# A head's sum of squares by two rounded products instead of one plain product, one slot later

## The chip, the cores and the metric

The kernel runs on one core of one Trainium2 chip. The metric is the device time of one execution in microseconds, from a few runs of the same program. Five engines work beside each other: TensorE (PE, with its weight loads as PEld), VectorE (DVE), ScalarE (ACT), GpSimd (POOL) and SyncE (SP), which issues the transfers.

## The reference

The program computes two blocks for 512 tokens of width 1024 in f32. The first has a state-space mixer, a chunked attention and a feed-forward part. The second has four layers, each with a mixer, a memory attention, an output projection and a feed-forward part. The mixer of the second of these layers (l = 1) is the differential attention, cut here to what matters:

```
for each of 4 heads, each block of 128 queries:
    a = softmax(q1 k1 + bias) - lam * softmax(q2 k2 + bias)
    o = a @ v                          # 256 features a head
o = _rmsnorm(o, g_head, HEAD_NORM_EPS) * (1.0 - lambda_init)

def _rmsnorm(x, g, eps):
    y = x * lax.rsqrt(jnp.mean(x * x, axis=-1, keepdims=True) + eps)
    return y * g
```

The mean over a head's 256 features is what the change is about.

## The kernel before

Everything stays on chip with features on the partitions and tokens along the free axis. An f32 operand of a large product is kept as two f32r tiles, its rounded value (whi, hh) and the remainder (wlo, hl), and each product is three f32r matmuls: high by high, low by high, high by low (L2539 to L2541, or L3254 to L3256). Weights stream by units of 1 MB: SyncE brings a unit into `raw` (two places), ScalarE rounds it into `whi` (L830), VectorE writes the remainder into `wlo` (L1501), and that frees the place in `raw`.

A mixer layer is written out by hand in slots. TensorE's queue holds for each unit n of the input projection four quarters (12 products of 512 columns, or 24 of 256), and in front of each quarter the attention work of that slot, s = 4n to 4n + 3; slots from 52 on lie between products of the output projection. VectorE and ScalarE hold the work of the same slots in the same order in their own queues. Every queue runs strictly in order, and semaphores alone tie them together. VectorE also has in its queue, between slots, the low half of the next unit (`low`, L1501) and the evictions of finished half units (`out_half`, L2465 and L2468), for which TensorE waits two slots later, before it writes the same bank again.

In the differential layer head hd starts at slot DZ[hd], with DZ = [20, 28, 36, 48]. By slots after that:

- 0 and 1: TensorE computes the scores of the two halves (L3235); VectorE adds the bias (L2356), takes maxima (L2360) and their negative, ngm (L2362). ScalarE takes the exponentials one slot later (L1404).
- 2 and 3: VectorE normalises and combines the two (L2369 to L2380).
- 5: TensorE transposes the ten blocks (L3222), and ScalarE copies them out (L1410).
- 6: TensorE multiplies by the values (L3214) into banks 6 and 7; ScalarE squares both (L1414).
- 7: VectorE adds the two squares (L2384), TensorE multiplies by a matrix of ones (L3206, which sums over the partitions), ScalarE takes the square root (L1419), VectorE the reciprocal (L2386).
- 8: VectorE multiplies the values by the gain and the reciprocal into `us` (L2391), and ScalarE rounds that into `act2` (L1423).
- 9: VectorE writes its remainder (L2260).

Within a slot VectorE's queue has the scores of a new head ahead of the work for slots 7, 8 and 9 of an older one. Slot 8 of heads 0 and 1 is slot 0 of heads 1 and 2. On TensorE the sum stands ahead of the scores. Scores of head 1 start with

```
for hd in at_slot(DZ, s, c):
    dve.wait_ge(S("d_z"), m + 1)                 # VectorE waits for the scores
...
pe.wait_ge(acc_free, g0 + evicted(unit_of(hd, 1), c))   # TensorE waits for q, k
```

and the transposes wait for the last of the probabilities (`pe.wait_ge(S("d_p"), 8 * (hd + 1))`). A normal unit starts with a wait for its low half, and its quarters 0 and 2 with a wait for the eviction of the same half of the unit before.

Of the kernel before, what the change touches and what calls it, by code (L numbers as in the profile page):

```python
# [23 lines left out]
F32 = mybir.dt.float32  # L24
F32R = mybir.dt.float32r
ALU = mybir.AluOpType
ACT = mybir.ActivationFunctionType
AX = mybir.AxisListType

P = 128  # L30
T = 512
# [41 lines left out]
def wq(i):  # L73
    return P * (i + 1)
# [28 lines left out]
KPV = [25, 29, 33, 37, 41, 45, 53, 56]  # L103

DZ = [20, 28, 36, 48]

def at_slot(table, s, after=0):

    return [h for h, n in enumerate(table) if n is not None and n + after == s]
# [29 lines left out]
def build(nc, A, out, ext_dram):  # L141
    with ExitStack() as ctx:
        sems = {}

        def S(name):
            if name not in sems:
                sems[name] = ctx.enter_context(nc.semaphore(name))
            return sems[name]
# [3 lines left out]
        def at(name, offset, shape, dt=F32):  # L152
            return nc.alloc_sbuf_tensor_at(name, shape, dt, offset=offset)
# [26 lines left out]
        US0 = place(2 * T * 4)  # L180
# [13 lines left out]
        ones = at("ones", place(P * 4), [P, P])  # L194
        negones = at("negones", place(P * 4), [P, P], F32R)
# [6 lines left out]
        hepsc = at("hepsc", place(4), [P, 1])  # L202
# [75 lines left out]
        def bank(b, w=BANK, off=0):  # L278
            return ps[:, b * BANK + off:b * BANK + off + w]
# [199 lines left out]
        dpt = at("dpt", TMP + 10240, [P, ZW])  # L479
        osq = [at(f"osq{i}", TMP + 15360 + 2048 * i, [P, T]) for i in range(2)]  # L480
        ors = at("ors", TMP + 19456, [P, T])
        dbias = at("dbias", TMP + 21504, [P, T])
        dneg = at("dneg", SQB0, [P, T])
        dist = at("dist", SQB0 + 2048, [P, T])
# [335 lines left out]
        def _(act):  # L820
            a = nc.scalar
# [573 lines left out]
            def differential_slot(s):  # L1395
                if s == DZ[0]:
                    act.wait_ge(S("d_lamsum"), 1)
                    a.activation(lam[:, 2:4], bank(3, 2), ACT.Exp).then_inc(S("d_lamexp"), 1)
                for c in range(2):
                    for hd in at_slot(DZ, s, 1 + c):  # L1400
                        act.wait_ge(S("d_ngm"), 2 * hd + c + 1)
                        for i in range(4):
                            z = dp[c][:, ZQ[i]:ZQ[i] + wq(i)]
                            a.activation(z, z, ACT.Exp, bias=ngm[:, c, i:i + 1],  # L1404
                                         accum_out=sums[:, c, i:i + 1]).then_inc(S("d_exp"), 1)
                for hd in at_slot(DZ, s, 5):
                    act.wait_ge(S("d_tr"), hd + 1)
                    if hd:
                        act.wait_ge(S("d_pv"), hd)
                    a.activation(dpt[:, :], ps[:, 0:ZW], ACT.Copy).then_inc(S("d_pt"), 1)  # L1410
                for hd in at_slot(DZ, s, 6):
                    act.wait_ge(S("d_pv"), hd + 1)
                    for d in range(2):
                        a.activation(osq[d][:, :], bank(6 + d), ACT.Square).then_inc(S("d_sq"), 1)  # L1414
                for hd in at_slot(DZ, s, 7):
                    act.wait_ge(S("d_ssum"), hd + 1)
                    if hd:
                        act.wait_ge(S("d_on"), 2 * hd)
                    a.activation(ors[:, :], bank(3), ACT.Sqrt, bias=hepsc[:, :], scale=1.0 / 256).then_inc(S("d_sd"), 1)  # L1419
                for hd in at_slot(DZ, s, 8):  # L1420
                    for d in range(2):
                        act.wait_ge(S("d_on"), 2 * hd + d + 1)
                        a.activation(act2[:, 2 * hd + d, 0, :], us[:, d, :], ACT.Copy).then_inc(mix_hi, 1)  # L1423
# [57 lines left out]
        def _(dve):  # L1481
            v = nc.vector
# [584 lines left out]
            for u in range(8):  # L2067
# [48 lines left out]
                if u >= 6:  # L2116
                    n = u - 6
# [99 lines left out]
            for c in range(4):  # L2217
                dve.wait_ge(mix_hi, 4 + c + 1)
                hi, lo = (act2[:, c, k, :].rearrange("p (c t) -> p t c", t=4) for k in range(2))
# [124 lines left out]
            def differential_slot(m0, s):  # L2344
                if s == DZ[0] - 5:
                    lambda_and_distance()
                for hd in at_slot(DZ, s, -1):
                    head_bias(hd)
                for c in range(2):
                    for hd in at_slot(DZ, s, c):  # L2350
                        m = 2 * hd + c
                        dve.wait_ge(S("d_z"), m + 1)
                        if hd and c == 0:
                            dve.wait_ge(S("d_tr"), hd)
                        for i in range(4):
                            v.tensor_tensor(dp[c][:, ZQ[i]:ZQ[i] + wq(i)], ps[:, ZQ[i]:ZQ[i] + wq(i)],  # L2356
                                            dbias[:, T - wq(i):T], ALU.add).then_inc(S("d_s"), 1)
                        for i in range(4):
                            dve.wait_ge(S("d_s"), 4 * m + i + 1)
                            v.tensor_reduce(mx[:, c, i:i + 1], dp[c][:, ZQ[i]:ZQ[i] + wq(i)], AX.X, ALU.max).then_inc(S("d_mx"), 1)  # L2360
                        dve.wait_ge(S("d_mx"), 4 * (m + 1))
                        v.tensor_scalar(ngm[:, c, :], mx[:, c, :], -1.0, None, ALU.mult).then_inc(S("d_ngm"), 1)  # L2362
                if s == DZ[0] + 1:
                    dve.wait_ge(S("d_lamexp"), 1)
                    link(v.tensor_tensor(lam[:, 4:5], lam[:, 3:4], lam[:, 2:3], ALU.subtract))
                    link(v.tensor_scalar(lam[:, 4:5], lam[:, 4:5], -LAMBDA_INIT, None, ALU.add))
                for hd in at_slot(DZ, s, 2):
                    dve.wait_ge(S("d_exp"), 8 * hd + 4)
                    link(v.reciprocal(rec[:, 0, :], sums[:, 0, :]))  # L2369
                    for i in range(4):  # L2370
                        z = dp[0][:, ZQ[i]:ZQ[i] + wq(i)]
                        v.tensor_scalar(z, z, rec[:, 0, i:i + 1], None, ALU.mult).then_inc(S("d_p"), 1)
                for hd in at_slot(DZ, s, 3):
                    dve.wait_ge(S("d_exp"), 8 * hd + 8)
                    link(v.reciprocal(rec[:, 1, :], sums[:, 1, :]))
                    link(v.tensor_scalar(rec[:, 1, :], rec[:, 1, :], lam[:, 4:5], None, ALU.mult))
                    for i in range(4):
                        z = slice(ZQ[i], ZQ[i] + wq(i))
                        dve.wait_ge(S("d_p"), 8 * hd + i + 1)
                        v.scalar_tensor_tensor(out=dp[0][:, z], in0=dp[1][:, z], scalar=rec[:, 1, i:i + 1],  # L2380
                                               in1=dp[0][:, z], op0=ALU.mult, op1=ALU.add).then_inc(S("d_p"), 1)
                for hd in at_slot(DZ, s, 7):
                    dve.wait_ge(S("d_sq"), 3 * hd + 2)
                    v.tensor_tensor(osq[0][:, :], osq[0][:, :], osq[1][:, :], ALU.add).then_inc(S("d_sq"), 1)  # L2384
                    dve.wait_ge(S("d_sd"), hd + 1)
                    link(v.reciprocal(ors[:, :], ors[:, :]))  # L2386
                for hd in at_slot(DZ, s, 8):
                    if hd:
                        dve.wait_ge(mix_hi, m0 + 2 + 2 * hd)
                    for d in range(2):  # L2390
                        v.scalar_tensor_tensor(out=us[:, d, :], in0=bank(6 + d), scalar=gdiff[:, d:d + 1], in1=ors[:, :],  # L2391
                                               op0=ALU.mult, op1=ALU.mult).then_inc(S("d_on"), 1)
                for hd in at_slot(DZ, s, 9):
                    for d in range(2):
                        mix_low(2 * hd + d, us[:, d, :], m0 + 2 + 2 * hd + d)
# [138 lines left out]
        def _(pe):  # L2534
            mm, tr = nc.tensor.matmul, nc.tensor.transpose
# [188 lines left out]
            for u in range(1, 8):  # L2724
# [7 lines left out]
                for c in range(2):  # L2732
# [6 lines left out]
                    else:  # L2739
                        if (u, c) == (6, 1):  # L2740
                            pe.wait_ge(acc_free, 6)
                        for t in (2 * c, 2 * c + 1):
                            for k in range(4):
                                f = 4 * (u - 6) + k
# [449 lines left out]
            def differential_slot(m0, s):  # L3194
                g0 = g_in(1)
                if s == DZ[0] - 1:
                    pe.wait_ge(S("d_lam"), 2)
                    pe.wait_ge(mix_ready, m0 + 1)
                    mm(bank(3, 2), ones[:, :], lam[:, 0:2], start=True, stop=True).then_inc(S("d_lamsum"), 1)
                for hd in at_slot(DZ, s, 7):  # L3200
                    pe.wait_ge(S("d_sq"), 3 * (hd + 1))
                    if hd:
                        pe.wait_ge(S("d_sd"), hd)
                    else:
                        pe.wait_ge(S("d_lamexp"), 1)
                    mm(bank(3), ones[:, :], osq[0][:, :], start=True, stop=True).then_inc(S("d_ssum"), 1)  # L3206
                for hd in at_slot(DZ, s, 6):
                    pe.wait_ge(S("d_pt"), hd + 1)
                    if hd:
# [14 lines left out]
                for c in range(2):  # L3224
                    for hd in at_slot(DZ, s, c):
# [8 lines left out]
                        for i in (0, 2, 3, 1):  # L3234
                            e = mm(ps[:, ZQ[i]:ZQ[i] + wq(i)], qp[hd % 2][:, c, P * i:P * i + P], kp[hd % 2][:, c, 0:wq(i)],  # L3235
                                   start=i != 2, stop=True, skip_group_check=True)
# [152 lines left out]
```

## Time and profile before

| | us |
|---|---|
| median of three runs | 2980.88 |
| the three runs | 2980.76, 2982.34, 2980.88 |
| profiled execution | 2980.96 |
| its span, first to last instruction | 2979.2 |
| TensorE busy | 2965.0 (100%) |
| VectorE busy | 2253.4 (76%) |
| ScalarE busy | 1461.9 (49%) |
| granted TensorE clock, mean | 0.999 |

The span is the stretch between the first and the last instruction on the core. The page shows busy time of each engine and its share of the span, a chain of waits followed back from the last instruction, and groups of instructions by line. A group can be asked for by line or tile, and a stretch can be listed in order of time. A matmul's duration in a listing overlaps its neighbours'; the distance from start to start is what it costs TensorE.

### The profile page before, as it was taken

What the parts mean: (1) busy time and instruction counts of PE and PEld (TensorE: products, weight loads), DVE (VectorE), ACT (ScalarE), POOL (GpSimd) and SP (SyncE); (2) the same over time, 40 slices, a digit from 0 to 9 for tenths busy, and PEclk for the clock granted to TensorE, in tenths of its full rate; (3) what the DMA queues carried; (4) which work ended last, traced back from release to release, by engine and by line L of the source; (5) the groups of instructions that cost most, each with busy time, mean ns of one, the idle gap of its engine ahead of it and who ended that gap; (6) DMA issues with size and microseconds to landing.
All of it is one profiled execution on the core that took longest, in us unless ns stands there. A gap on an engine that the chain in (4) does not pass through costs nothing.

```text
span 2979.2 us, 47840 instructions
## 1 busy us (share of the span) xinstructions
PE 2965.0 (100%) x18717; PEld 2651.8 (89%) x18717; DVE 2253.4 (76%) x2775; ACT 1461.9 (49%) x2143; POOL 58.6 (2%) x148
## 2 busy tenths in 40 slices
PE   9999999999999999999999999999999999999999
PEld 8779999888889999878899998788999878899998
DVE  7978888566759887566598874658988557588984
ACT  4476555454345555444455553325555344355554
POOL 6100000000000000000000000000000000000000
PEclk9999999999999999999999999999999999999999
DMA  6122332342133333221333333223333222232332
GB/s 189 49 72 91 100 125 94 111 136 71 56 101 99 99 106 100 92 63 57 104 102 99 99 107 106 85 66 115 102 99 106 93 85 66 62 114 99 105 101 78
DMA packets 256759, 283.30 MB, mean 95 GB/s; under 512 B 11938, under 2 KB 229216, under 8 KB 256616
## 3 DMA queue, kind: packets, MB, share of 16 engines
q1 hardware_dynamic: 256504, 281.28, 29.5%
q8 instruction: 102, 1.67, 0.2%
q14 instruction: 41, 0.34, 0.0%
q10 hardware_dynamic: 112, 0.02, 0.0%
HBM read 279.16 MB, written 4.73 MB: 95 GB/s over the span
## 4 chain that ended last, share of the span: by engine, by line
PE 92%; DVE 4%; POOL 1%; issue 1%; ACT 1%; DMA 0%; ACTq 0%; DVEq 0%; POOLq 0%; SPq 0%
PE ps L2914 40%; PE ps L2539 14%; PE ps L2541 14%; PE ps L2540 14%; PE ps L3268 1%; PE ps L3269 1%; PE ps L3270 1%; PE ps L3175 1%; PE ps L3235 1%; PE ps L3214 1%; PE ps L3254 1%; PE ps L3256 1%; PE ps L3255 1%; PE ps L3104 1%; PE ps L3124 1%
## 5 line engine op out<-in xcount | busy, mean ns | idle before, releaser
L830 ACT ACTIVATE whi<-raw 128x2048 fp32r<-128x2048 f32 (+2 forms) x144 | 246.5, 1712 | 488.2 <-PE ps L2541 409.5
L1501 DVE TENSOR_TENSOR wlo<-raw,whi 128x2048 fp32r<-128x2048 f32 (+2 forms) x144 | 293.5, 2038 | 223.7 <-ACT whi L830 223.4
L2914 PE MATMUL ps<-th,wh 128*128 128x256 f32 x1600 | 453.7, 284 | 0.6 <-DVE wl L1590 0.5
L2914 PE MATMUL ps<-tl,wh 128*128 128x256 f32 x1600 | 452.7, 283 | 0.0
L2914 PE MATMUL ps<-th,wl 128*128 128x256 f32 x1600 | 452.7, 283 | 0.0
L2539 PE MATMUL ps<-hh,whi 128*128 128x512 f32 x896 | 357.3, 399 | 0.2 <-DVE wlo L1899 0.2
L2541 PE MATMUL ps<-hh,wlo 128*128 128x512 f32 x896 | 349.7, 390 | 0.0
L2540 PE MATMUL ps<-hl,whi 128*128 128x512 f32 x896 | 349.3, 390 | 0.0
L2914 PE MATMUL ps<-hh,wh 128*128 128x256 f32 x1200 | 340.1, 283 | 0.2
L2914 PE MATMUL ps<-hh,wl 128*128 128x256 f32 x1200 | 339.6, 283 | 0.0
L2914 PE MATMUL ps<-hl,wh 128*128 128x256 f32 x1200 | 339.6, 283 | 0.0
L2914 PEld LDWEIGHTS ps<-th,wh 128*128 128x128 f32 x1600 | 307.0, 192 | 2.3 <-DVE wl L1590 1.1
L2914 PEld LDWEIGHTS ps<-tl,wh 128*128 128x128 f32 x1600 | 307.1, 192 | 0.2
L2914 PEld LDWEIGHTS ps<-th,wl 128*128 128x128 f32 x1600 | 307.1, 192 | 0.0
L2914 PEld LDWEIGHTS ps<-hh,wh 128*128 128x128 f32 x1200 | 230.3, 192 | 1.1 <-DVE gs L1641 0.8
L2914 PEld LDWEIGHTS ps<-hl,wh 128*128 128x128 f32 x1200 | 230.4, 192 | 0.2
L2914 PEld LDWEIGHTS ps<-hh,wl 128*128 128x128 f32 x1200 | 230.3, 192 | 0.0
L2539 PE MATMUL ps<-acth,whi 128*128 128x512 f32 x560 | 218.4, 390 | 0.0
L2540 PE MATMUL ps<-actl,whi 128*128 128x512 f32 x560 | 218.1, 389 | 0.0
L2541 PE MATMUL ps<-acth,wlo 128*128 128x512 f32 x560 | 217.9, 389 | 0.0
L2539 PEld LDWEIGHTS ps<-hh,whi 128*128 128x128 f32 x896 | 168.3, 188 | 38.0 <-issue 4.7
L2541 PEld LDWEIGHTS ps<-hh,wlo 128*128 128x128 f32 x896 | 168.2, 188 | 36.0
(516 smaller groups left out, 6658.6 us busy)
## 6 DMA issues: line engine op xcount, KB each, us to landing
raw<-in_w_ffn_in SPq DMA_DIRECT2D x88, 1024.0 KB, 5.1
raw<-in_w_in SPq DMA_DIRECT2D x59, 1024.0 KB, 5.3
raw<-in_w_ffn_out SPq DMA_DIRECT2D x40, 1024.0 KB, 5.1
raw<-in_w_o SPq DMA_DIRECT2D x32, 640.0 KB, 4.4
raw<-in_w_gate SPq DMA_DIRECT2D x11, 1024.0 KB, 5.3
raw<-in_w_up SPq DMA_DIRECT2D x11, 1024.0 KB, 5.3
raw<-in_w_down SPq DMA_DIRECT2D x10, 1024.0 KB, 5.0
raw<-in_w_out SPq DMA_DIRECT2D x4, 1024.0 KB, 5.5
```

The lines of the kernel that those rows point to most:

```text
L830: a.activation(whi[:, slot, 0:n], raw[:, slot, 0:n], ACT.Copy).then_inc(hi_made, 1)
L1501: v.tensor_tensor(wlo[:, u % 2, 0:n], raw[:, u % 2, 0:n], whi[:, u % 2, 0:n].bitcast(F32), ALU.subtract).then_inc(lo_made, 1)
L2539: mm(dst, wh, xh, start=first, stop=False, skip_group_check=True)
L2540: mm(dst, wh, xl, start=False, stop=False, skip_group_check=True)
L2541: return mm(dst, wl, xh, start=False, stop=last, skip_group_check=True)
L2914: e = mm(bank(b, HALF), wgt[:, q, w], xx, start=start and k == 0 and m == 0, stop=k == KD // 2 - 1 and m == 2, skip_group_check=True)
L3104: e = mm(bank(b + r, MEM, MEM * i), mq[rows, f, t:t + P], km[rows, l, f, :], start=i == 0, stop=True, skip_group_check=True)
L3124: e = mm(ps[64 * r:64 * r + 64, o:o + 256], vm[:, l, j, MD * h:MD * h + MD], mt[:, j, 256 * r:256 * r + 256], start=j == 0, stop=j == 1, s ...
L3175: e = tr(ps[:, o:o + P], stick[:, ZQ[i] + P * j:ZQ[i] + P * j + P], ident[:, :])
L3214: e = mm(bank(6 + d, T - P * j, P * j), vp[hd % 2][:, j, P * d:P * d + P], dpt[:, ZK[j]:ZK[j] + wk(j)], start=j == 0, stop=j == 3, skip_gr ...
L3235: e = mm(ps[:, ZQ[i]:ZQ[i] + wq(i)], qp[hd % 2][:, c, P * i:P * i + P], kp[hd % 2][:, c, 0:wq(i)], start=i != 2, stop=True, skip_group_che ...
L3254: mm(dst, hs, whi[:, slot, w], start=k == 0, stop=False, skip_group_check=True)
```

## The change

The sum of the two squares is rounded to f32r (`osum_hi`), its remainder is computed by two more VectorE operations (`osum_lo`), and TensorE multiplies both by a matrix of minus ones in f32r, adding up in one bank; the square root takes the opposite sign in its scale. The product, the square root and the reciprocal move from slot DZ + 7 to the table DSUM = [28, 36, 44, 55], which is DZ + 8 for heads 0 to 2 and DZ + 7 for head 3. The two new tiles lie where `us` lies.

```diff
+DSUM = [28, 36, 44, 55]
...
+        osum_hi, osum_lo = (at(f"osum_{n}", US0 + 2048 * k, [P, T], F32R) for k, n in enumerate(("hi", "lo")))
...
 # ScalarE
-                for hd in at_slot(DZ, s, 7):
+                for hd in at_slot(DSUM, s):
                     act.wait_ge(S("d_ssum"), hd + 1)
                     if hd:
                         act.wait_ge(S("d_on"), 2 * hd)
-                    a.activation(ors[:, :], bank(3), ACT.Sqrt, bias=hepsc[:, :], scale=1.0 / 256).then_inc(S("d_sd"), 1)
+                    a.activation(ors[:, :], bank(3), ACT.Sqrt, bias=hepsc[:, :], scale=-1.0 / 256).then_inc(S("d_sd"), 1)
...
 # VectorE
                 for hd in at_slot(DZ, s, 7):
-                    dve.wait_ge(S("d_sq"), 3 * hd + 2)
-                    v.tensor_tensor(osq[0][:, :], osq[0][:, :], osq[1][:, :], ALU.add).then_inc(S("d_sq"), 1)
+                    dve.wait_ge(S("d_sq"), 4 * hd + 2)
+                    v.tensor_tensor(osum_hi[:, :], osq[0][:, :], osq[1][:, :], ALU.add).then_inc(S("d_sq"), 1)
+                    dve.wait_ge(S("d_sq"), 4 * hd + 3)
+                    link(v.tensor_tensor(osq[0][:, :], osq[0][:, :], osum_hi[:, :].bitcast(F32), ALU.subtract))
+                    v.tensor_tensor(osum_lo[:, :], osq[0][:, :], osq[1][:, :], ALU.add).then_inc(S("d_sq"), 1)
+                for hd in at_slot(DSUM, s):
                     dve.wait_ge(S("d_sd"), hd + 1)
                     link(v.reciprocal(ors[:, :], ors[:, :]))
...
 # TensorE
-                for hd in at_slot(DZ, s, 7):
-                    pe.wait_ge(S("d_sq"), 3 * (hd + 1))
+                for hd in at_slot(DSUM, s):
                     if hd:
                         pe.wait_ge(S("d_sd"), hd)
                     else:
                         pe.wait_ge(S("d_lamexp"), 1)
-                    mm(bank(3), ones[:, :], osq[0][:, :], start=True, stop=True).then_inc(S("d_ssum"), 1)
+                    pe.wait_ge(S("d_sq"), 4 * hd + 3)
+                    mm(bank(3), negones[:, :], osum_hi[:, :], start=True, stop=False)
+                    pe.wait_ge(S("d_sq"), 4 * hd + 4)
+                    mm(bank(3), negones[:, :], osum_lo[:, :], start=False, stop=True).then_inc(S("d_ssum"), 1)
```

`link` makes VectorE wait for the end of the instruction it wraps.

## Rows read from the trace of the kernel before

**Rows 1.** The page: chain of waits by engine, and one line of DMA issues.

```profile
PE 92%; DVE 4%; POOL 1%; issue 1%; ACT 1%; DMA 0%; ACTq 0%; DVEq 0%; POOLq 0%; SPq 0%
...
raw<-in_w_in SPq DMA_DIRECT2D x59, 1024.0 KB, 5.3
```

**Rows 2.** The chain from 1300 to 1450 us: start, duration, what.

```profile
1320.13 0.86 PE ps L3206 x2
...
1330.87 1.68 DVE dp L2356 x4
...
1335.52 2.20 DVE wlo L1501
1337.72 0.60 DVE qp L2468
...
1340.11 1.95 DVE dp L2380 x4
1342.10 1.31 PE ps L3222 x10
```

**Rows 3.** Timeline of TensorE at 254 us: start, duration, engine, line, operation.

```profile
254.60 0.40 PE L2591 MATMUL ps<-diag_hi,negones 128*128 128x512 f32 x1
254.83 0.39 PE L2592 MATMUL ps<-diag_lo,negones 128*128 128x512 f32 x1
255.06 0.39 PE L2539 MATMUL ps<-hh,whi 128*128 128x512 f32 x1
```

**Rows 4.** Timeline of VectorE, slots 27 to 29, head 0; idle before in brackets.

```profile
1318.58 0.69 DVE L2384 TENSOR_TENSOR osq<-osq,osq 128x512 f32<-128x512 f32 x1 [4.21 <-ACT osq L1414]
1321.74 3.35 DVE L2386 RECIPROCAL ors<-ors 128x512 f32<-128x512 f32 x1 [2.47 <-ACT ors L1419]
1325.13 0.69 DVE L2468 SCALAR_TENSOR_TENSOR kp<-ps,rs 128x512 f32<-128x512 f32 x1
1325.94 1.68 DVE L2356 TENSOR_TENSOR dp<-ps,dbias 128x128 f32<-128x128 f32 x4
...
1329.31 1.40 DVE L2391 SCALAR_TENSOR_TENSOR us<-ps,gdiff,ors 128x512 f32<-128x512 f32 x2
1330.87 1.68 DVE L2356 TENSOR_TENSOR dp<-ps,dbias 128x128 f32<-128x128 f32 x4 [0.16 <-PE ps L3235]
```

**Rows 5.** Timeline, head 1 in slots 36, 37 and 41: VectorE, VectorE, TensorE.

```profile
1362.44 1.40 DVE L2391 SCALAR_TENSOR_TENSOR us<-ps,gdiff,ors 128x512 f32<-128x512 f32 x2
1364.10 1.68 DVE L2356 TENSOR_TENSOR dp<-ps,dbias 128x128 f32<-128x128 f32 x4 [0.26 <-PE ps L3235]
...
1375.34 1.31 PE L3222 MATMUL ps<-ident,dp 128*128 128x128 f32 x10
```

**Rows 6.** Timeline, head 2: the eviction in slot 46, TensorE's scores of slot 48.

```profile
1397.08 0.68 DVE L2468 SCALAR_TENSOR_TENSOR kp<-ps,rs 128x512 f32<-128x512 f32 x1
...
1400.83 2.32 PE L3235 MATMUL ps<-kp,qp 128*128 128x128 f32 x8
```

**Rows 7.** Timeline, head 3 in slot 55: VectorE, then TensorE.

```profile
1430.22 0.69 DVE L2384 TENSOR_TENSOR osq<-osq,osq 128x512 f32<-128x512 f32 x1 [2.58 <-ACT osq L1414]
...
1432.36 1.02 PE L3206 MATMUL ps<-osq,ones 128*128 128x512 f32 x2
```

**Rows 8.** Timeline of ScalarE, slots 27 and 28.

```profile
1318.49 1.28 ACT L1419 ACT_TABLE_LOAD   x1
1321.02 0.69 ACT L1419 ACTIVATE ors<-ps,hepsc 128x512 f32<-128x512 f32 x1 [1.24 <-PE ps L3206]
1323.84 1.91 ACT L830 ACTIVATE whi<-raw 128x2048 fp32r<-128x2048 f32 x1 [2.13 <-PE ps L2541]
```

**Rows 9.** Timeline of TensorE: the first product of slot 32.

```profile
1338.88 0.39 PE L2539 MATMUL ps<-hh,whi 128*128 128x512 f32 x1
```

**Rows 10.** TensorE's longest wait, and windows (busy us, granted clock, DMA share, GB/s).

```profile
2.13 2.82 PE L2615 MATMUL ps<-ident 128*128 128x128 f32 x12 [2.13 <-POOL ident L690]
...
0.00:4.00 4.00, 1.87 (x9) 1.88 (x10) 0.00 (x0) 1.23 (x1) 1.93 (x18) 1.00 0.45 145
```

## The prediction

> **What bounds the kernel now.** I read three views in this order. First the page's chain of waits: TensorE holds 92% of it and VectorE 4% [rows 1]. So an instruction put on TensorE's queue costs its issue step, and other engines cost only where TensorE's next wait ends on them. Second, the same chain cut to the differential layer's attention (1300 to 1450 us), to find those places. From 1330.87 to 1342.05 us the chain leaves TensorE and runs along VectorE without a break: score additions, maxima, the low half of a weight unit (L1501), an eviction (L2468), the probabilities (L2380); then the ten transposes L3222 start at 1342.10 [rows 2]. That is slots 29 to 33. The next head repeats it: additions at 1364.10, transposes at 1375.34 [rows 5]. The two stretches follow DZ[1] = 28 and DZ[2] = 36, the slots in which DSUM puts the sum of the head before. Third, the timelines of VectorE and ScalarE around each of the four sums, for who is idle there.
>
> **TensorE's own work.** The plain product over osq is two f32 passes and takes 0.86 us of the chain [rows 2]. The two rounded products have a twin in the trace: L2591 and L2592, the same weights and 512 columns, from 254.60 to the next product at 255.06, 0.46 us [rows 3]. Per head that is 0.86 - 0.46 = 0.40 us less on the engine that bounds, 1.60 us over four heads if nothing else moved. The sign in the square root's scale costs nothing: it is an operand of the same instruction.
>
> **VectorE's added work.** Two more 128x512 operations a head. One takes 0.69 us, and each has to wait for the one before it. In slot 27 the first starts at 1318.58, so the low part ends near 1318.58 + 3 x 0.73 = 1320.8 us; VectorE was idle until 1321.74 there, and the reciprocal is gone from this slot [rows 4]. TensorE asks for the low part only in slot 28, after 1322.7. Free for heads 0 to 2. Head 3 keeps its slot (48 + 7 = 55): its sum started at 1430.22, so the remainder is ready near 1432.41; TensorE comes at 1432.36 for the high part and 0.23 us later for the low one [rows 7]. It fits by about 0.2 us; at worst, if the wait stands in front of both products, it costs 0.1 us. I take 0.
>
> **The reciprocal, moved by a slot: the term that decides.** It takes 3.35 us, and 1321.74 to 1325.13 is 3.39 us to the next operation [rows 4]. Before, it ran in slot 27 in time in which VectorE had little else to do (idle 2.47 us just ahead of it). Now it stands in slot 28 behind the next head's additions, maxima and ngm and ahead of the two multiplications into us. Head 0, on the trace's own time up to the sum:
>
> - Slot 28 on TensorE comes 0.86 us earlier (the plain product left slot 27) and its scores start 0.46 us later (the two products go first): 0.40 us early. VectorE's additions waited for those scores (1325.94), so they start at 1325.54, and what stood at 1329.31, now the reciprocal, at 1328.91 [rows 4].
> - ScalarE has the square root ready by then: the weight conversion ahead of it, at 1323.84, moves to about 1323.0 and takes 1.91, the table load 1.28, the root 0.69: 1326.9 us [rows 8]. The table load loses its cover of waiting time, but 2.0 us are left.
> - Reciprocal to 1332.30. The two multiplications take the 1.40 us of their row, of which the next start hides 0.08: the second scores' additions start at 1333.62, where they stood at 1330.87 [rows 4]. That is 2.75 us late.
> - From there VectorE's queue has no gap in which to recover [rows 2], so everything behind is 2.75 us late: the low half for slot 32, the eviction that slot 32 also waits for, and the probabilities. ScalarE's copies and exponentials follow the same clock: its exponentials of the second half would end near 1340.1, and the reciprocal that needs them comes at about 1342.4.
> - TensorE wants slot 32 at 1338.88 - 0.40 = 1338.48 [rows 9]. The eviction, 1337.72 + 0.60 = 1338.32 before [rows 2], now ends at about 1341.1. So there is a new wait of 2.6 us at the first product of slot 32, then 2.7 us of products, then a wait of 1.0 us at the transposes, which start at 1342.10 + 2.75 = 1344.85.
>
> Head 1 by the same sum: what stood at 1362.44 starts at 1362.04, the reciprocal ends at 1365.43, the additions start at 1366.75 instead of 1364.10, 2.65 us late; there too the transposes start where the last probability ends, at 1375.34 [rows 5]. Head 1 loses 2.65 us. The 0.40 us of both heads are inside these figures.
>
> Head 2 has no new scores behind it (DSUM 44, DZ[3] = 48). The reciprocal pushes the multiplications, the low halves and the eviction of 1397.08. That eviction releases the scores of slot 48, which stood at 1400.83 [rows 6]. It ended near 1397.77; all in front of it moves 0.86 earlier and takes 3.39 more: 1400.30, against 1400.43 at which TensorE arrives. Cover 0.13 us: it keeps its 0.40 us, and I bound the loss at 0.4 us. Head 3 keeps its 0.40 us.
>
> The weight loads: the low halves that free raw come up to 2.8 us later, so SyncE issues those transfers later; a unit lands 5.3 us after its issue [rows 1]. The transfer that L1501 of slot 29 releases at 1337.72 is first read by the conversion at the head of slot 36, whose multiplications stand at 1362.44 [rows 5]. Nothing.
>
> Sum: 2.75 + 2.65 - 0.40 - 0.40 = +4.6 us. The profiled execution took 2980.96 us (span 2979.2), 0.08 us above the median of 2980.88, so the forecast is 2985.6 us.
>
> **A rule against the small price.** The longest wait of TensorE in the trace is 2.13 us, before its first product, and the granted clock of the first 4 us is 1.00, the 2.4 GHz level [rows 10]. No row shows a longer one. The Trainium skill (TensorE: Matmul & The Clock Gate, Part 1: The HAM clock gate) says the default is throttled: idle TensorE falls to half its clock, and activity releases it. No wait in this trace goes with a fall, so no row bears out that the new waits would cause one; it is rival B.
>
> **The rivals.**
> A. The reciprocal's delay is absorbed and only the products count: 2980.96 - 1.60 = 2979.4 us. For it: most of the layer runs with VectorE well ahead. Against it: VectorE's rows from 1330.87 to 1342.10 are back to back and end in the transposes [rows 2]. It decides if 2.75 us of idle lay in that stretch.
> B. TensorE's clock halves after the waits. The slot between the two waits would take twice 2.7 = 5.4 us, end at 1346.5 instead of 1344.85, and cost 1.7 us a head: 2989.0 us. For it: the new waits, 2.6 and 1.0 us close together, are longer than any before. Against: the engine is busy before and between them.
> C. The tight covers fail: slot 48 arrives before its eviction (0.4 us), the remainder of head 3 is late (0.1 us), and instructions restarted after the two new waits expose their weight loads (0.2 us each): up to 2986.5 us. For it: margins of 0.1 and 0.2 us.
> D. VectorE takes the rounded parts slower than plain additions and ScalarE's root comes too late, so that the reciprocal starts late: it needs over 2.0 us of delay; one more table load (1.28 us) is not enough. A full second load beyond that, 0.6 us a head: 2986.8 us.
>
> **Chances.** The forecast 0.70, with its own range 2985.0 to 2986.2; C 0.12; B 0.07; A 0.06; D 0.05. The bound of a measurable difference, 0.2%, is 5.96 us: 2974.9 and 2986.8. Faster than the first is almost excluded, 0.02. Slower than the second: B, the edge of D, and a spread of the median of about 1 us (the three runs span 1.6), 0.14 together. Range for 8 in 10: 2984.2 to 2987.3, leaving out A and B.
>
> **What would show it.** In the profile after: a wait of about 2.6 us on TensorE at the first product of slots 32 and 40, and one of 1.0 us at L3222 (both put down to VectorE), twice; the reciprocal right behind ngm, with no idle before it, for heads 0 and 1; two one-pass products in place of L3206's two passes; the low part ended before slot 28; no wait at slot 48; the granted clock at 1.00 through all of it. I am wrong if slots 32 and 40 start unhindered, or if the reciprocal stands ahead of the additions, or if the time grows in another layer, which the change does not touch.

## The result and the profile after

The changed kernel takes 2986.84 us (median of 18 runs, 2986.14 to 2987.99), the kernel before 2980.91 us (18 runs, 2980.27 to 2982.34): 5.93 us or 0.20% more. The ratio is 1.002, 95% interval 1.0013 to 1.0026. The forecast was 2985.6 us, with a range of 2984.2 to 2987.3. The profiled execution took 2986.38 us, its span is 2984.7.

The page after: busy time by engine, and the chain of waits by engine.

```profile
PE 2964.8 (99%) x18717; PEld 2652.2 (89%) x18717; DVE 2259.5 (76%) x2783; ACT 1461.2 (49%) x2143; POOL 57.9 (2%) x148
...
PE 91%; DVE 5%; POOL 1%; issue 1%; ACT 1%; DMA 0%; SPq 0%; ACTq 0%; DVEq 0%
```

TensorE's busy time is the same to 0.2 us while the span grew by 5.5, so the net growth is waiting. Two things cancel in the busy time: 1.6 us of products are saved, and slower products, shown below, put about as much back. (The same kernel with a short operation for the reciprocal, e3_short_reciprocal, whose clock stayed up, has 2963.1 us.) The view of TensorE's waits, asked for the whole span, has two entries that the kernel before had not, and one that has grown from 0.3 us (columns: who waited for whom, us in total, times, longest):

```profile
PE ps L2545 <- DVE qp L2474: 2.6, 1, 2.6
...
PE ps L2545 <- DVE v_pairs L2471: 2.1, 1, 2.1
...
PE ps L3230 <- DVE dp L2382: 0.7, 1, 0.7
```

L2474 and L2471 are the evictions for which slots 32 and 40 wait, L3230 the transposes. VectorE's timeline of head 0, the answer to [rows 4]:

```profile
1318.81 0.69 DVE L2386 TENSOR_TENSOR osum_hi<-osq,osq 128x512 fp32r<-128x512 f32 x1 [4.21 <-ACT osq L1416]
1319.54 0.69 DVE L2388 TENSOR_TENSOR osq<-osq,osum_hi 128x512 f32<-128x512 f32 x1
1320.26 0.69 DVE L2389 TENSOR_TENSOR osum_lo<-osq,osq 128x512 fp32r<-128x512 f32 x1
...
1325.74 1.68 DVE L2358 TENSOR_TENSOR dp<-ps,dbias 128x128 f32<-128x128 f32 x4 [1.93 <-PE ps L3243]
...
1329.11 3.35 DVE L2392 RECIPROCAL ors<-ors 128x512 f32<-128x512 f32 x1
1332.49 1.41 DVE L2397 SCALAR_TENSOR_TENSOR us<-ps,gdiff,ors 128x512 f32<-128x512 f32 x2
1333.81 1.67 DVE L2358 TENSOR_TENSOR dp<-ps,dbias 128x128 f32<-128x128 f32 x4
```

Everything here is 0.23 us later than before from something ahead of the layer (1318.81 against 1318.58). Taken from that first addition, the additions of the second scores stand at 15.00 us where they stood at 12.29: 2.71 late. The reciprocal has no idle time in front of it. Ahead of the scores VectorE now stands idle for 1.93 us; before, the reciprocal and an eviction filled the time up to them. ScalarE's square root ended 2.0 us before the reciprocal started:

```profile
1326.40 0.69 ACT L1421 ACTIVATE ors<-ps,hepsc 128x512 f32<-128x512 f32 x1
```

TensorE's timeline: the two products, the last product of slot 31, the first of slot 32 and the transposes of head 0.

```profile
1322.91 0.40 PE L3212 MATMUL ps<-osum_hi,negones 128*128 128x512 f32 x1
1323.15 0.39 PE L3214 MATMUL ps<-osum_lo,negones 128*128 128x512 f32 x1
1323.38 2.32 PE L3243 MATMUL ps<-kp,qp 128*128 128x128 f32 x8
...
1338.44 0.39 PE L2547 MATMUL ps<-hh,wlo 128*128 128x512 f32 x1
1341.41 0.47 PE L2545 MATMUL ps<-hh,whi 128*128 128x512 f32 x1 [2.58 <-DVE qp L2474]
...
1345.04 1.31 PE L3230 MATMUL ps<-ident,dp 128*128 128x128 f32 x10 [0.66 <-DVE dp L2382]
```

And the same engine in slot 40, head 1, where a second thing shows:

```profile
1377.25 0.77 PE L2545 MATMUL ps<-hh,whi 128*128 128x512 f32 x1 [2.06 <-DVE v_pairs L2471]
...
1378.67 0.63 PE L2545 MATMUL ps<-hh,whi 128*128 128x512 f32 x1
1379.10 0.63 PE L2546 MATMUL ps<-hl,whi 128*128 128x512 f32 x1
...
1381.14 0.39 PE L2546 MATMUL ps<-hl,whi 128*128 128x512 f32 x1
1381.37 0.39 PE L2547 MATMUL ps<-hh,wlo 128*128 128x512 f32 x1
1381.60 1.25 PE L3230 MATMUL ps<-ident,dp 128*128 128x128 f32 x10
```

The first products behind that wait start 0.43 us apart instead of 0.23. Windows of the same trace (busy us of PE, PEld, DVE, ACT, POOL, then the granted clock, DMA share and GB/s):

```profile
1341.40:1345.00 3.60, 2.97 (x12) 2.16 (x12) 3.53 (x11) 0.76 (x1) 0.00 (x0) 1.00 0.85 264
1374.00:1377.20 3.20, 1.19 (x10) 0.99 (x9) 3.19 (x4) 3.20 (x10) 0.00 (x0) 0.98 0.00 0
1377.20:1380.70 3.50, 3.45 (x9) 2.76 (x10) 3.41 (x10) 0.79 (x1) 0.00 (x0) 0.53 0.83 266
1380.70:1384.00 3.30, 3.30 (x21) 2.87 (x20) 2.92 (x3) 1.11 (x1) 0.00 (x0) 1.00 0.11 36
```

The granted clock went to its 1.2 GHz level (0.53 in that window, 0.98 and 1.00 around it) after the engine had been idle, and came back while it worked. It stayed at 1.00 behind the longer wait of head 0. The Trainium skill (TensorE: Matmul & The Clock Gate, Part 1: The HAM clock gate) says that idle time throttles the array and that activity releases it; this trace agrees for head 1 and not for head 0.

The transposes of head 1 end up waiting for TensorE's own products. VectorE's last probability operation started at 1378.89 and took 1.94, so it ended at 1380.83; with the kernel before, the transposes followed such an end by 0.05 us. Here they start at 1381.60. That is 0.7 us from the clock.

Head 2's eviction and head 3's low part, with what TensorE starts behind them:

```profile
1405.75 0.68 DVE L2474 SCALAR_TENSOR_TENSOR kp<-ps,rs 128x512 f32<-128x512 f32 x1
...
1406.61 2.37 PE L3243 MATMUL ps<-kp,qp 128*128 128x128 f32 x8
...
1437.52 0.69 DVE L2389 TENSOR_TENSOR osum_lo<-osq,osq 128x512 fp32r<-128x512 f32 x1
...
1438.43 0.39 PE L3214 MATMUL ps<-osum_lo,negones 128*128 128x512 f32 x1
```

The eviction ended at 1406.43, 0.18 us ahead of the scores; the low part at 1438.21, 0.22 us ahead. Both covers held.

From five marks in each trace the whole can be laid out: head 0's first addition of squares, the transposes in slots 33 and 41, the scores of slot 48, the first sum product of slot 55. Below, us between marks, and the difference to the kernel before ([rows 4], [rows 2], [rows 5], [rows 6], [rows 7]):

| | to slot 33 | to slot 41 | to slot 48 | to slot 55 |
|---|---|---|---|---|
| before | 23.52 | 33.24 | 25.49 | 31.53 |
| changed | 26.23 (+2.71) | 36.56 (+3.32) | 25.01 (-0.48) | 31.59 (+0.06) |
| forecast | +2.75 | +2.65 | -0.40 | 0 |

The four differences add up to 5.61 us. With the 0.23 us from ahead of the layer, and the 0.40 us that head 3 saves behind the last mark, that makes 5.44; the two profiled executions differ by 5.42.

### The profile page after: what moved, and what is told of

It reads as the page before. It is cut to its first block, busy times and chain, and to the rows that moved or that the text cites. A ratio compares the mean times of both kernels' runs of the same rounds, so it can differ in the third digit from the quotient of the medians.

```text
span 2984.7 us, 47846 instructions
## 1 busy us (share of the span) xinstructions
PE 2964.8 (99%) x18717; PEld 2652.2 (89%) x18717; DVE 2259.5 (76%) x2783; ACT 1461.2 (49%) x2143; POOL 57.9 (2%) x148
## 4 chain that ended last, share of the span: by engine, by line
PE 91%; DVE 5%; POOL 1%; issue 1%; ACT 1%; DMA 0%; SPq 0%; ACTq 0%; DVEq 0%
PE ps L2920 40%; PE ps L2545 14%; PE ps L2547 14%; PE ps L2546 14%; PE ps L3276 1%; PE ps L3277 1%; PE ps L3278 1%; PE ps L3181 1%; PE ps L3222 1%; PE ps L3110 1%; DVE wlo L1503 1%; PE ps L3130 1%; PE ps L3119 0%; PE ps L3262 0%; PE ps L3263 0%
```

## The experiments

Theory Q: the loss is the reciprocal's new place, between the scores of the next head in VectorE's queue. Theory C: the longer waits that follow let TensorE's clock fall, which adds to it. Rivals: P, the split sum itself costs (more work and waits on VectorE and TensorE); R, ScalarE's root behind a weight conversion and a table load holds up the slot. The kernel before ran beside these on the same chip: 2980.79 us (33 runs) for the first four, 2980.92 us (27 runs) for the others.

**The products alone (e1_products_alone).**

```diff
-DSUM = [28, 36, 44, 55]
+DSUM = [27, 35, 43, 55]
```

> The two rounded products stay, the move is undone: DSUM = [27, 35, 43, 55], so product, root and reciprocal are back in slot DZ + 7. Theory Q (the loss is the reciprocal's new place in VectorE's queue): the loss goes. Per head TensorE spends 0.40 us less, but in slot 27 it now arrives at the sum about 0.6 us before the low part is written (three dependent 0.69 us operations after the squares), so heads 0 to 2 win back nothing or lose 0.2 us each and head 3 keeps its 0.40: 2980.5 to 2981.5 us, and no wait of TensorE over 1 us in slots 27 to 56. Rival P (the split sum itself costs: more VectorE work, more waits): the loss stays, near 2985 us or more. Rival C (the clock): no long wait, so nothing to fall; same number as Q.

Measured: 2981.54 us (11 runs), ratio 1.0002, interval 0.9993 to 1.0011. TensorE's waits between 1250 and 1470 us:

```profile
PE ps L3214 <- DVE osum_lo L2389: 1.2, 3, 0.4
PE ps L3230 <- DVE dp L2382: 0.3, 1, 0.3
```

The loss is gone with the move, so P falls as the cause of it; the time is at the upper end of what was expected. What the split sum costs at its old place is the wait for the low part, 0.4 us in each of three slots. It eats the saving, and delays the reciprocal: the marks for slots 33 and 41 stand 0.30 and 0.29 us later than before.

**The move alone (e2_move_alone).** The plain product over the sum, at DSUM's slots. TensorE's part against the changed kernel; VectorE's two added operations and the sign in the root's scale go too.

```diff
...
-                    pe.wait_ge(S("d_sq"), 4 * hd + 3)
-                    mm(bank(3), negones[:, :], osum_hi[:, :], start=True, stop=False)
-                    pe.wait_ge(S("d_sq"), 4 * hd + 4)
-                    mm(bank(3), negones[:, :], osum_lo[:, :], start=False, stop=True).then_inc(S("d_ssum"), 1)
+                    pe.wait_ge(S("d_sq"), 3 * (hd + 1))
+                    mm(bank(3), ones[:, :], osq[0][:, :], start=True, stop=True).then_inc(S("d_ssum"), 1)
```

> The move stays, the products go back to one plain f32 product over the sum, in slot DZ + 8 (head 3: DZ + 7). Theory Q: head 0's reciprocal starts at 1329.31 on the time of the kernel before instead of 1328.91, so the next work is 3.15 us late, head 1's 3.05 us, heads 2 and 3 nothing: about 2987.1 us, 0.4 us a head above the changed kernel before any fall of the clock. A wait of about 3.0 us in slots 32 and 40, longer than in the changed kernel, so with theory C (a long wait lowers the granted clock) a stretch of 1.2 GHz at one or both, up to 1.7 us each. Rival P: close to before, 2981 us.

Measured: 2987.82 us (11 runs, 2986.9 to 2989.34), ratio 1.0023, interval 1.0013 to 1.0032. The marks stand 3.74 and 3.70 us late where 3.15 and 3.05 were expected, and the clock accounts for the rest, 0.6 us each: in this trace both slots run most of their products 0.43 us apart. TensorE's first product of slot 32 waited as long as in the changed kernel, not the 3.0 us expected, since TensorE came later by the 0.40 us that it no longer saved:

```profile
1341.06 0.77 PE L2542 MATMUL ps<-hh,whi 128*128 128x512 f32 x1 [2.57 <-DVE qp L2471]
```

The move alone explains the loss and more; the two products then give 1.56 us back (2987.82 against the 2986.26 of e4_changed_again, run beside it), where four times 0.40 makes 1.6.

**A short operation for the reciprocal (e3_short_reciprocal).** This kernel leaves out the normalisation of heads 0 and 1.

```diff
-                    link(v.reciprocal(ors[:, :], ors[:, :]))
+                    if hd < 2:
+                        link(v.tensor_tensor(ors[:, :], ors[:, :], ors[:, :], ALU.mult))
+                    else:
+                        link(v.reciprocal(ors[:, :], ors[:, :]))
```

> The changed kernel with a 0.69 us multiplication in place of the 3.35 us reciprocal for heads 0 and 1 (their normalisation is left out; heads 2 and 3 keep theirs). Theory Q: VectorE's stretch to the transposes is 2.66 us shorter than in the changed kernel, 0.1 us late for head 0 and about even for head 1, so no wait in slots 32 and 40, a wait at the transposes of 0.3 to 0.5 us as before, granted clock 1.00 throughout; heads 2 and 3 keep 0.40 us each: 2980.2 us. Rival R (ScalarE's table load and root behind the weight conversion hold up slot 28): the root's end does not move, so most of the loss stays, 2984 us or more.

Measured: 2979.79 us (11 runs), ratio 0.9996, interval 0.9987 to 1.0005. The two marks are 0.04 late and 0.05 us early. The same slots, the same queue, the same root and table load, 2.66 us less in one operation, and 6.5 us of time are gone. R falls. Two heads with 2.66 us each make 5.3 us; the rest is again the clock's share, for this trace shows 1.00 from 1300 to 1450 us.

**The changed kernel again (e4_changed_again).** No edit.

> The changed kernel once more, for its trace. Theory Q: both waits in slots 32 and 40 are there again, 2.6 and 2.1 to 2.2 us, with the transposes of head 1 near 2.9 to 3.3 us late. Theory C: where the clock falls it is in the products behind one of the two waits; whether at head 0, head 1, both or neither differs from run to run, and each fall costs up to 0.8 us with what the second wait covers (the stepped 0.43 us products eat the cover of the wait at the transposes first). Median 2986.8 us. Rival: the fall belongs to head 1 alone, for a reason in its stretch: then it is there again, at the same place.

Measured: 2986.26 us (11 runs, 2985.48 to 2987.64). In this trace the clock fell at both places. Windows over slots 32 and 40:

```profile
1341.10:1344.80 3.70, 3.67 (x9) 2.92 (x10) 3.62 (x11) 0.78 (x1) 0.00 (x0) 0.55 0.84 274
...
1377.60:1382.00 4.40, 4.32 (x13) 3.39 (x14) 4.29 (x13) 0.83 (x1) 0.00 (x0) 0.66 0.75 238
```

In slot 40 the products had run again at 0.23 us apart before the clock fell:

```profile
1377.68 0.47 PE L2545 MATMUL ps<-hh,whi 128*128 128x512 f32 x1 [2.05 <-DVE v_pairs L2471]
...
1378.45 0.39 PE L2545 MATMUL ps<-hh,whi 128*128 128x512 f32 x1
...
1379.23 0.63 PE L2545 MATMUL ps<-hh,whi 128*128 128x512 f32 x1
```

The waits were 2.57 and 2.05 us, the same as in the first trace, so the length of a wait alone does not decide whether the clock falls. Head 0's mark is 3.49 us late instead of 2.71: the fall cost 0.78 us there. Head 1's is 3.00 us late, and the stretch behind it is only 0.15 us shorter than before instead of 0.40, since the clock was still low at the transposes: 0.65 us together. The rival that it belongs to head 1's stretch falls.

**Two reciprocals (e5_two_reciprocals).**

```diff
+                    if hd < 2:
+                        link(v.reciprocal(osq[1][:, :], ors[:, :]))
                     link(v.reciprocal(ors[:, :], ors[:, :]))
```

> The changed kernel with one more reciprocal (into a tile that is free by then) ahead of the real one for heads 0 and 1. Theory Q: each adds 3.39 us to VectorE's stretch and all of it reaches TensorE: the waits in slots 32 and 40 grow from 2.6 and 2.1 to about 6.0 and 5.5 us, transposes about 6.1 us late a head: 2980.8 + 6.1 + 6.0 - 0.8 = 2992.1 us with the clock untouched. Theory C (a longer wait, a surer fall to 1.2 GHz): both waits are followed by products at 0.43 us from start to start, about 0.8 us more each, 1.7 at most: 2993.5 to 2995.5 us. Rival (part of the added time finds cover): under 2990 us.

Measured: 2994.85 us (4 runs, 2993.07 to 2995.38), ratio 1.0045, interval 1.003 to 1.006. First product of slot 32, and a window over it:

```profile
1344.48 0.77 PE L2547 MATMUL ps<-hh,whi 128*128 128x512 f32 x1 [5.96 <-DVE qp L2476]
```

```profile
1345.00:1349.00 4.00, 4.00 (x11) 3.12 (x10) 3.93 (x11) 0.23 (x1) 0.00 (x0) 0.50 0.78 260
```

The marks are 7.71 and 7.53 us late. The first reciprocal's 2.75 and 2.65, the second's 3.39 each, leave 1.6 and 1.5 us for the clock: with both slots all through at 1.2 GHz a fall costs close to the 1.7 us that the prediction gave as its price. That was right as a price for a whole slot.

**Fillers while it waits (e8_fillers).**

```diff
+                    if l == 1 and n in (8, 10):
+                        pe.wait_ge(S("d_sd"), 1 if n == 8 else 2)
+                        for _ in range(10 if n == 8 else 9):
+                            mm(bank(3), negones[:, :], hh[:, 0, :], start=True, stop=True, skip_group_check=True)
                     unit_ready(u0 + n)
```

> The changed kernel with ten and nine products whose result nobody reads put on TensorE's queue in front of slots 32 and 40, some 2.3 and 2.0 us of the time in which it waits there. Theory Q with C: the waits shrink to under 0.5 us, the transposes of heads 0 and 1 still start at the end of the last probabilities, because VectorE's stretch is the same, but the granted clock stays 1.00 through both places and the 0.7 to 0.8 us that a fall cost is gone: 2985.3 to 2985.9 us, some 0.5 to 1.2 us under the changed kernel. Rival (the clock falls for the array's work before the wait, not for the idle): a fall shows up again and the time is 2986.5 us or more.

Measured: 2985.29 us (11 runs, 2984.86 to 2986.07), ratio 1.0015, interval 1.0006 to 1.0024. The fillers, the wait that is left at slot 32, the wait at the transposes of head 1, and a window over slot 40:

```profile
1338.64 2.49 PE L3291 MATMUL ps<-hh,negones 128*128 128x512 f32 x10
1341.38 0.47 PE L2545 MATMUL ps<-hh,whi 128*128 128x512 f32 x1 [0.25 <-DVE qp L2474]
...
1380.85 1.31 PE L3230 MATMUL ps<-ident,dp 128*128 128x128 f32 x10 [0.65 <-DVE dp L2382]
```

```profile
1377.20:1380.80 3.60, 3.00 (x13) 2.16 (x12) 3.53 (x11) 0.77 (x1) 0.00 (x0) 1.00 0.88 276
```

Against the kernel before on its own chip that is 4.37 us more, where the changed kernel had 5.47 (e4_changed_again) and 5.93: nineteen useless products win 1.1 to 1.6 us. The clock stays at 1.00 in both slots of the trace, and the marks are what Q alone asks for: +2.70, +2.60, -0.41, +0.05. The rival (the work ahead of the wait lowers the clock) falls, and theory C is borne out. In the three traces with both waits left open (the changed kernel twice, and the move alone) the clock fell behind five of six; with the waits filled it fell behind neither. Idle time was needed for a fall but was not enough for one, as head 0 of the first trace shows.

**The sum inside the quarter (e6_sum_inside_quarter).** DSUM = [27, 35, 43, 55]; for heads 0 to 2 TensorE's part stands behind the first three products of the quarter.

```diff
...
+                    if k % 4 == 0:
+                        for hd in sums:
+                            sum_of_squares(hd)
...
```

> Both rounded products in slot DZ + 7, but for heads 0 to 2 three products behind the slot's start, so that the low part is written when TensorE asks for it. Theory Q: the 0.4 us waits of the version with the products alone go; heads 0 and 1 end even or 0.2 us late by VectorE's stretch, heads 2 and 3 keep 0.40 us: 2980.3 us, against 2981.5 for the products at the slot's start. Rival (the sum's distance from the reciprocal decides): the reciprocal starts 0.7 us later and the transposes of heads 0 and 1 are 0.7 us late each: 2981.5 us or more.

Measured: 2979.94 us (11 runs, 2979.02 to 2982.46), ratio 0.9997, interval 0.9988 to 1.0006. The waits for the low part are gone. The marks are 0.16 and 0.27 us early, better than the "even or 0.2 us late" expected. The reciprocal starts 0.3 us later in its stretch than in the kernel before, but the scores come earlier, and VectorE's gaps ahead of the second additions, 0.16 and 0.26 us [rows 4, 5], are gone.

**The low halves later (e7_low_halves_later).** The same, and VectorE writes the low halves of us for heads 0 and 1 behind the next head's probabilities.

```diff
...
+DLOW = [31, 39, 45, 57]
...
-                for hd in at_slot(DZ, s, 9):
+                for hd in at_slot(DLOW, s):
...
```

> The version before plus one move: the low halves of us (L2262, 1.20 us of VectorE's stretch) of heads 0 and 1 go from slots 29 and 37 to behind the next head's probabilities in slots 31 and 39. Theory Q: that shortens the stretch to the transposes by 1.2 us a head, so TensorE no longer waits there (0.5 and 0.1 us from start to start before) and all four heads keep their 0.40 us: 2980.8 - 0.57 - 1.6 = 2978.6 us, below the kernel before. Rival (another wait is close behind, the eviction for slot 34 or 42): 2979.5 us or more.

Measured: 2979.01 us (11 runs, 2978.01 to 2981.44), ratio 0.9994, interval 0.9985 to 1.0003. TensorE waits for nothing between 1250 and 1470 us. VectorE in head 1's stretch, the moved operation behind the probabilities:

```profile
1370.76 1.94 DVE L2383 SCALAR_TENSOR_TENSOR dp<-dp,rec,dp 128x128 f32<-128x128 f32 x4
1372.62 1.28 DVE L2263 TENSOR_TENSOR act<-us,act 128x512 fp32r<-128x512 f32 x2
```

The marks are 0.89 and 0.53 us early (the two waits of 0.5 and 0.1 us and the 0.40 us of each head were expected), then 0.43. The median is 1.9 us under the kernel before and 0.4 above the expectation; the interval of the ratio still holds 1.

## Why the prediction was right, and where it was off

**The reciprocal, moved by a slot.** Right in mechanism and size; it is the term that makes up the loss. It was worked out as 2.75 and 2.65 us late for heads 0 and 1; the trace where the clock stays up (e8_fillers) has 2.70 and 2.60, and head 0 of the changed kernel 2.71. Shortening the operation takes the loss away, undoing the move takes it away, and doubling it brings 7.71 and 7.53 us, the 3.39 us of a second one and the clock's share: the queue position is shown to be the cause.

**Where the wait appears.** Right for head 0. The first product of slot 32 waited 2.58 us (2.6 forecast). The transposes waited 0.66 us by the profile, or 0.82 from start to start (the last product started at 1343.99 and takes 0.23, the transposes at 1345.04), where 1.0 was forecast. For head 1 the prediction took the same two waits over, which is not what came: slot 40 waits for another eviction (v_pairs, L2471), for 2.06 us instead of 2.6, and what is left waits at the transposes, 0.65 us in e8_fillers. In the changed kernel's trace the slow products covered that second wait whole. The sum is the same, for both waits end where VectorE's stretch ends.

**TensorE's own work.** Right: the pair starts at 1322.91, the scores at 1323.38, 0.47 us against the 0.46 of the twin. Per head 0.40 us is saved, and the stretches without a wait show it.

**VectorE's added work, the tight covers.** Right: the low part ended 0.22 us ahead of its product in slot 55, the eviction 0.18 us ahead of slot 48. Rival C of the prediction did not come; its third part, a restart that costs 0.2 us, shows as 0.31 us from the first product of slot 32 to the second instead of 0.23, and the second wait covers it.

**The clock (rival B), put at nothing.** The prediction held it apart as a rival with a chance of 0.07, counted it in neither the sum nor the range, and named a granted clock of 1.00 all through as a sign of being right, since no row of the kernel before showed a fall. That sign did not come. The clock falls in most places where the new wait stands: at one of two in the first trace, at both in e4_changed_again and e2_move_alone. A fall cost 0.6 to 0.8 us there rather than 1.7, because the second wait, for the probabilities, covers the rest, and because the clock was low for only part of the products. That is the term missing from the sum. The time grew by 5.93 us against 4.6 forecast; the 1.3 us between them is about two such falls (1.2 to 1.6), and the kernel with the fillers, whose trace has no fall, took 2985.29 us, 4.37 more than before.

How often the clock falls can't be counted without a trace, but each run's mean clock, known to a thousandth, points the same way. It was 0.998 or less in 16 of the 29 runs of the changed kernel, in 7 of 11 with the move alone and in all 4 with two reciprocals, against 5 of 60 of the kernel before that ran beside them and none of 11 with the fillers.

**The number.** 2986.84 us lies inside the range of 2984.2 to 2987.3 but outside the narrower 2985.0 to 2986.2, to which the prediction gave 0.70. The wide range left out B, and its upper end had room for rival C and for the spread of the median. What filled that room was the clock. That the number still fell inside is in part luck.

**The other rivals.** A (delay absorbed) is excluded: head 0's mark is 2.71 us late. D (ScalarE's root late) is excluded by e3_short_reciprocal, and by the trace itself: the root ended at 1327.09, 2.0 us ahead of the reciprocal, as forecast, and no wait stands there.

## What to carry to other kernels

In queues written out by hand, a move by one slot is not a move by time but into another neighbourhood: ask which long operation now stands between what the bounding engine's next wait depends on, and add up the idle gaps of that stretch; if there are none, the operation arrives at the bounding engine (here 2.7 of 3.35 us; the second one of e5_two_reciprocals arrived in full). A gain on the bounding engine (here 0.40 us a head) is easily lost to a wait of a few us, and such a wait may cost more than its length when TensorE's clock falls behind it (here 0.6 to 0.8 us more). If the operands of a moved product are late by less than a slot, put the product a few instructions into the slot instead of one slot later.

## What the runs showed of the hardware

The granted clock of TensorE fell to its 1.2 GHz level behind waits of 2.1 and 2.6 us in a kernel that otherwise keeps the engine busy 99% of the time, and was back at 1.00 while the next products ran (from 1380.70 us on in the first trace). Behind waits of 6.0 and 5.4 us (e5_two_reciprocals) the whole slot ran low. In slot 40 of e4_changed_again it fell only after the products had started again. It did so behind the same wait in one run (0.55 after 2.57 us) and not in another (1.00 after 2.58 us). With products that nobody reads put into the wait it stayed at 1.00, and the kernel took 1.1 to 1.6 us less.
